# Two order edits in a transformer trunk: when the attention output is loaded and split, and where one variance product stands on TensorE

## The chip, the cores and the metric

The kernel runs on one core of one Trainium2 chip. Times are device microseconds (us) of one launch. A kernel is timed as the median of several runs; where a profile is read, the rows come from one profiled execution with a span of its own.

## What is computed

One inference step of two layers over 1,032 token columns (1,024 prompt positions and 8 decoding rows), with a model width of 1,024. Each layer is a token mixer, a layer norm, a gated feed-forward part with a causal convolution of width 3, and a second layer norm:

```python
xp = layer_norm(ALPHA * xp + hp, ln_g[i, 0], ln_b[i, 0])      # hp = attention output @ w_o (+ b_o in layer 1)
fp, sp = conv_ffn(xp, zeros_prev, w_up[i], conv_w[i], conv_b[i], w_down[i])
xp = layer_norm(ALPHA * xp + fp, ln_g[i, 1], ln_b[i, 1])

def layer_norm(x, g, b):
    xf = x.astype(jnp.float32)
    mu = xf.mean(-1, keepdims=True)
    var = jnp.square(xf - mu).mean(-1, keepdims=True)
    return ((xf - mu) * lax.rsqrt(var + LN_EPS) * g + b).astype(x.dtype)
```

Everything behind the mixer is called the trunk here. It runs twice, once for each layer; both edits are in it.

## The kernel before

**Arithmetic.** Every large product is made of three passes. Each operand is split into a rounded high part and the rest: ScalarE copies the high part (`w_hi`, `t_h_hi`, `x_hi`), VectorE or GpSimd subtracts it to get the low part (`w_lo`, `t_h_lo`, `x_lo`), and TensorE adds high times high, high times low and low times high in PSUM (lines 101 to 103, in the helper `product`). The model dimension lies on partitions, the tokens on the free axis, in three chunks of 352, 352 and 328 columns (`CHUNKS`, c = 0, 1, 2).

**Blocks.** The trunk is a list of blocks (`trunk_slots`, `slots`). Block b multiplies one weight piece of 128 x 1024 with one chunk: 8 x 3 matmuls. Blocks 0 to 23 are the output projection `w_o`, kind "o": blocks 0 to 7 are chunk 0 (m = 0 to 7), 8 to 15 chunk 1, 16 to 23 chunk 2. Block 24 is the first of the feed-forward part; it reads the normalised chunk 0. All engines walk through the same list, each with its own instructions in program order; semaphores join them.

**Weights.** `raw`, `w_hi` and `w_lo` are rings of three slots (`RING`). SyncE issues the load of block b (`load_w`, line 1288, 512 KB) once the low part of block b - 3 is done. In its block b, ScalarE first copies the high part of block b + 2 (line 1337), once TensorE has finished block b - 1. GpSimd makes the low parts of even blocks (line 1455), VectorE those of odd blocks (line 1536, in its block b for block b + 2, b odd).

**Attention output.** The mixer leaves it in DRAM (`o_scr`). For every chunk it is loaded in four quarters q = 0 to 3 of 128 x 2 x 352 values (`load_o`, line 1279) into staging columns, and each quarter is split by ScalarE (line 1342) and VectorE (line 1542). The four staging places are the same for every chunk, so the load of quarter q of chunk c waits until quarter q of chunk c - 1 is split:

```python
need(sp, s_olo, 4 * (c - 1) + q + 1)      # line 1278, on SyncE's queue
```

Before the change, the loads of chunk c + 1 stand behind `load_w` at m = 5 of chunk c (line 1301), and all four splits stand in ScalarE's and VectorE's block m = 6 (lines 1424 and 1670).

**Norm steps.** When the eight tiles of a chunk are projected, its layer norm is worked off beside the blocks of the next chunk. `NORM` lists its steps with an offset, and `norm_block(stage, what, at)` gives the block; stage 0 is chunk 0 behind the output projection, which ends with block 7, so `end` is 8. For stage 0: the mean product on TensorE ahead of block 10 (line 1770); "center" k = 0 to 3 on VectorE in blocks 10 to 13 (line 1604) and "square" k on ScalarE right behind in the same block (lines 1376 and 1381); the sums of squares on VectorE ("add", line 1611, blocks 12 to 14, "fold", line 1616, block 15); the variance product on TensorE (line 1774), square root on ScalarE (line 1387) and reciprocal on VectorE (line 1621), all with block 16; then "scale" (VectorE, line 1627), "high" (ScalarE, line 1401), "affine" (GpSimd, line 1488) and "low" (VectorE, line 1633), k = 0 to 3, one block apart, from blocks 17, 17, 18 and 19. Block 24 waits for all four "low".

Within a block, ScalarE does: weight copy, quarter copies if any, norm steps. VectorE does: weight split (odd b), quarter splits if any, norm steps, then the residual addition of the tile of block b - 1 (lines 1559 and 1562). GpSimd does its weight split (even b), adds the tile to the running sum (line 1470), then norm steps.

Of the kernel before, what the change touches and what calls it, by code (L numbers as in the profile page):

```python
# [50 lines left out]
NCH = len(CHUNKS)  # L51
# [4 lines left out]
def f32(ap):  # L56
    return ap.bitcast(F32)


def need(eng, sem, count):  # L60

    if isinstance(count, int) and count <= 0:
        return
    eng.wait_ge(sem, count)
# [1033 lines left out]
def stage_of(kind, c):  # L1098
    return c if kind == "o" else NCH + c


def stage_end(stage):


    return KT * (stage + 1) if stage < NCH else NCH * KT + FFN_BLOCKS * (stage - NCH + 1)
# [11 lines left out]
def norm_block(stage, what, at):  # L1117


    end = stage_end(stage)  # L1120
    if what == "mean":
        return end + 2 + (10 if stage == 2 else 0)
    if stage == 0:
        return end + 2 + at
    if what == "affine":
        at += 0.5
    return (26, 50)[stage - 1] + int(2 * at) if stage < NCH else end + 2 + int(2 * at)
# [11 lines left out]
def mixer_b_constants(zb):  # L1139


    views, at = {}, 0
    flat = zb[:, :, :].rearrange("p m c -> p (m c)")
    for name, size in (("cos", T), ("sin", T), ("mask", 2 * P), ("ident", P), ("nsink", NH), ("bias", 3 + PAIRS)):
        views[name] = flat[:, at:at + size]
        at += size
    return views


def trunk(nc, x_hi, x_lo, banks, ring, zb, dram, layer):  # L1150
# [5 lines left out]
    with ctx:  # L1156
# [62 lines left out]
        def pieces(b):  # L1219
            kind, c, m, j = slots[b]  # L1220
            return DOWN_PIECES[j] if kind == "d" else KT
# [17 lines left out]
        def stored(stage):  # L1239

            return final and stage >= NCH

        def o_part(c, q):


            n = CHUNKS[c][1]
            stage = (h_hi, h_lo)[q // 2][:, 16 + 2 * (q % 2):18 + 2 * (q % 2), 0:n]
            a = 8 * (c % 2) + 2 * q
            return f32(stage), h_hi[:, a:a + 2, 0:n], h_lo[:, a:a + 2, 0:n]
# [7 lines left out]
        def two(ap, k, n):  # L1257


            return ap[:, 2 * k:2 * k + 2, 0:n]  # L1260
# [4 lines left out]
        @block.sync  # L1265
        def _(sp):
            def source(kind, m, j):
                if kind == "o":
                    return dram["w_o"][m]
                if kind in "gu":  # L1270
                    return dram["w_up"][2 * m + j]
                if kind == "p":
                    return dram["w_b"][AHEAD[m]]
                return dram["w_down"][3 * m + j]

            def load_o(c, q):
                off, n = CHUNKS[c]
                need(sp, s_olo, 4 * (c - 1) + q + 1)
                sp.dma_start(o_part(c, q)[0],
                             dram["o_scr"].rearrange("(m p) t -> p m t", p=P)[:, 2 * q:2 * q + 2, off:off + n]  # L1280
                             ).then_inc(o_in[q], 16)

            def load_w(b):
                kind, c, m, j = slots[b]
                n = pieces(b) * P
                if b >= RING:
                    need(sp, s_wlo[b % 2 if RING % 2 == 0 else 1 - b % 2], (b - RING) // 2 + 1)
                sp.dma_start(raw[:, b % RING, 0:n], source(kind, m, j)[:, 0:n]).then_inc(w_in[b % RING], 16)

            load_w(0)  # L1290
            for q in range(4):
                load_o(0, q)
            if biased:
                sp.dma_start(bias[:, :], dram["bias_o"]).then_inc(s_bias, 16)
            for b in range(1, n_blocks):
                kind, c, m, j = slots[b]
                load_w(b)
                if b == 3:
                    for dst, name in ((state[:, :, :, :], "state"), (taps[:, :, :], "taps"), (ln[:, :, :, :], "ln")):
                        sp.dma_start(dst, dram[name][layer]).then_inc(s_const, 16)  # L1300
                if kind == "o" and m == 5 and c + 1 < NCH:
                    for q in range(4):
                        load_o(c + 1, q)
                if stored(stage_of("d", c - 1)) and kind == "g" and m == 14:
                    store_y = c - 1
                    off, n = CHUNKS[store_y]
                    need(sp, s_y, KT * (NCH + store_y + 1))
                    sp.dma_start(dram["yT"].rearrange("(m p) t -> p m t", p=P)[:, :, off:off + n],
                                 z[(NCH + store_y) % 2][:, :, 0:n]).then_inc(s_out, 16)
            if not final:  # L1310
                views = mixer_b_constants(zb)
                sp.wait_ge(s_blk, N_BLOCKS)
                for part, name in (("cos", "cos"), ("sin", "sin"), ("mask", "mask_b"), ("ident", "ident"), ("bias", "bias_b")):
                    sp.dma_start(views[part], dram[name]).then_inc(s_next, 16)
                sp.dma_start(views["nsink"], dram["sinks"].partition_broadcast(P)).then_inc(s_next, 16)
            need(sp, s_save, NCH * FT)
            sp.dma_start(dram["gT"][layer], gtail[:, :, :]).then_inc(s_out, 16)
            if final:
                off, n = CHUNKS[NCH - 1]
                for k in range(KT // 2):  # L1320
                    need(sp, s_y, KT * (N_STAGES - 1) + k + 1)
                    need(sp, s_yodd, k + 1)
                    sp.dma_start(two(dram["yT"].rearrange("(m p) t -> p m t", p=P)[:, :, off:off + n], k, n),
                                 two(z[(N_STAGES - 1) % 2], k, n)).then_inc(s_out, 16)
            need(sp, s_out, 16 * (1 + NCH - 1 + KT // 2 if final else 1))
            if not final:
                sp.wait_ge(s_next, 16 * 6)

        @block.scalar
        def _(act):  # L1330
# [8 lines left out]
            def split_o(c, q):  # L1339
                src, hi, _ = o_part(c, q)  # L1340
                act.wait_ge(o_in[q], 16 * (c + 1))
                act.copy(hi, src).then_inc(s_ohi, 1)
# [75 lines left out]
            for b in range(n_blocks):  # L1418
                kind, c, m, j = slots[b]
                if b + 2 < n_blocks:  # L1420
                    split(b + 2)
                if biased and tile_before(b) and tile_before(b)[0] == "o":
                    add_bias(b, *tile_before(b)[1:])
                if kind == "o" and m == 6 and c + 1 < NCH:
                    for q in range(4):
                        split_o(c + 1, q)
                if kind == "g" and m > 1:
                    high_h(c, m - 2)
                if kind == "u":
                    gate_rows(b, c, m)  # L1430
                    if m > 0:
                        silu(c, m - 1)
                if kind == "d" and m == 0 and j == 0:
                    silu(c, FT - 1)
                    high_h(c, FT - 2)
                if kind == "d" and m == 0 and j == 1:
                    high_h(c, FT - 1)
                if b == 8:
                    act.wait_ge(s_const, 48)
                for stage, what, k in norm_steps(b):  # L1440
                    norm(stage, what, k)
# [89 lines left out]
        def _(dve):  # L1531
# [7 lines left out]
            def split_o(c, q):  # L1539
                src, hi, lo = o_part(c, q)  # L1540
                dve.wait_ge(s_ohi, 4 * c + q + 1)
                dve.tensor_tensor(lo, src, f32(hi), ALU.subtract).then_inc(s_olo, 1)  # L1542
# [123 lines left out]
            for b in range(n_blocks):  # L1666
                kind, c, m, j = slots[b]
                if b % 2 == 1 and b + 2 < n_blocks:
                    split(b + 2)
                if kind == "o" and m == 6 and c + 1 < NCH:  # L1670
                    for q in range(4):
                        split_o(c + 1, q)
                if kind == "u":
                    convolve(c, m)
                    if m > 0:
                        gate(b - 1, c, m - 1)
                if kind == "d" and m == 0 and j == 0:
                    gate(b, c, FT - 1)
                if b == 8:
                    dve.wait_ge(s_const, 48)  # L1680
                if b == ROWS_AT:
                    sample_rows()
                for stage, what, k in norm_steps(b):
                    norm(stage, what, k)
                for tile in tile_due(b):
                    residual(*tile)
# [963 lines left out]
```

## Time and profile before

| | us |
|---|---|
| median of 3 runs | 3184.15 (3181.24 to 3186.31) |
| the profiled execution, its own time | 3190.73 |
| its span | 3189.1 |
| TensorE busy in the span | 3086.4 (97%) |
| VectorE, ScalarE, GpSimd busy | 1598.9, 1528.1, 1542.6 (50%, 48%, 48%) |
| mean granted TensorE clock | 0.984 of full |

TensorE is busy nearly all the time, so the time of the kernel is TensorE's work plus the places where it stands still; about 100 us of the span are such places. "Idle" in a row is time in which an engine had nothing to run, with the instruction that ended it. A clock of 1.00 in a row is 2.4 GHz, 0.50 is 1.2 GHz.

### The profile page before, as it was taken

The page shows a single profiled execution, that of the slowest core. Times are in us where ns is not written, and L with a number is a line of the kernel's source. Part 1 is how long each engine was busy: PE and PEld are TensorE (multiplying, and loading weights), DVE is VectorE, ACT ScalarE, POOL GpSimd, SP SyncE. Part 2 cuts the span into 40 slices and gives each one's busy share as a digit, 9 for nine tenths or more (in the row PEclk, how much of TensorE's full clock was granted, in tenths as well). Part 3 has the DMA queues.
Part 4 walks back from the last instruction along what each step waited for, and adds up shares of the span by engine and source line. Part 5 has one row for each costly group of instructions (what it writes and reads, how often), then busy time and mean ns, then how long its engine had stood idle before and what let it go on. Part 6 is the DMA issues. An engine that isn't in the chain of part 4 may idle for free. (4 is left out here: it accounts for less than half of the span.)

```text
span 3189.1 us, 54992 instructions
## 1 busy us (share of the span) xinstructions
PE 3086.4 (97%) x21141; PEld 2974.7 (93%) x21141; DVE 1598.9 (50%) x3409; ACT 1528.1 (48%) x3235; POOL 1542.6 (48%) x1277
## 2 busy tenths in 40 slices
PE   8999999999999889999999999999899999999997
PEld 8999999999999859999999999988799999999997
DVE  3234434344343446664463465589756653433543
ACT  4555555555555424553453353367655543533542
POOL 4344443444444315665564465454256654554663
PEclk9999999999999989999999999999899999999998
DMA  6676676776776474444444444311244444444542
GB/s 225 241 262 229 226 259 230 244 258 209 267 256 222 173 289 137 144 134 128 137 133 141 137 144 143 119 37 43 79 164 134 140 128 136 156 133 143 163 145 96
DMA packets 134212, 540.80 MB, mean 170 GB/s; under 512 B 24336, under 2 KB 48544, under 8 KB 131120
## 3 DMA queue, kind: packets, MB, share of 16 engines
q1 hardware_dynamic: 133440, 536.51, 50.0%
q8 instruction: 169, 2.77, 0.4%
q14 instruction: 91, 0.75, 0.1%
q0 software_dynamic: 224, 0.26, 0.0%
q10 hardware_dynamic: 288, 0.52, 0.0%
HBM read 497.55 MB, written 216.85 MB: 224 GB/s over the span
## 5 line engine op out<-in xcount | busy, mean ns | idle before, releaser
L1337 ACT CAST w_hi<-raw 128x1024 fp32r<-128x1024 f32 (+1 forms) x459 | 471.5, 1027 | 847.7 <-PE bank L103 796.9
L101 PE MATMUL bank<-x_hi,w_hi 128*128 128x352 f32 (+1 forms) x2208 | 711.9, 322 | 5.6 <-POOL w_lo L1455 4.3
L102 PE MATMUL bank<-x_lo,w_hi 128*128 128x352 f32 (+1 forms) x2208 | 705.9, 320 | 0.0
L103 PE MATMUL bank<-x_hi,w_lo 128*128 128x352 f32 (+1 forms) x2208 | 702.5, 318 | 0.0
L1536 DVE TENSOR_TENSOR w_lo<-raw,w_hi 128x1024 fp32r<-128x1024 f32 (+1 forms) x229 | 320.2, 1398 | 737.7 <-ACT w_hi L1337 737.7
L1455 POOL TENSOR_TENSOR w_lo<-raw,w_hi 128x1024 fp32r<-128x1024 f32 (+1 forms) x230 | 546.8, 2378 | 277.0 <-ACT w_hi L1337 277.0
L101 PE MATMUL a_gemm<-x_hi,a_w_hi 128*128 128x352 f32 (+1 forms) x1728 | 561.0, 325 | 11.2 <-DVE x_lo L645 11.2
L102 PE MATMUL a_gemm<-x_lo,a_w_hi 128*128 128x352 f32 (+1 forms) x1728 | 553.7, 320 | 0.0
L103 PE MATMUL a_gemm<-x_hi,a_w_lo 128*128 128x352 f32 (+1 forms) x1728 | 551.7, 319 | 0.0
L101 PE MATMUL bank<-t_h_hi,w_hi 128*128 128x352 f32 (+1 forms) x1440 | 465.0, 323 | 7.9 <-POOL t_h_lo L1475 5.7
L103 PE MATMUL bank<-t_h_hi,w_lo 128*128 128x352 f32 (+1 forms) x1440 | 463.4, 322 | 0.0
L102 PE MATMUL bank<-t_h_lo,w_hi 128*128 128x352 f32 (+1 forms) x1440 | 460.6, 320 | 0.0
L101 PEld LDWEIGHTS bank<-x_hi,w_hi 128*128 128x128 f32 x2208 | 414.7, 188 | 8.7 <-POOL w_lo L1455 5.3
L102 PEld LDWEIGHTS bank<-x_lo,w_hi 128*128 128x128 f32 x2208 | 415.3, 188 | 1.6
L103 PEld LDWEIGHTS bank<-x_hi,w_lo 128*128 128x128 f32 x2208 | 415.0, 188 | 0.0
L577 POOL TENSOR_TENSOR a_w_lo<-a_raw,a_w_hi 128x1024 fp32r<-128x1024 f32 x72 | 172.3, 2392 | 387.3 <-ACT a_w_hi L445 387.3
L101 PEld LDWEIGHTS a_gemm<-x_hi,a_w_hi 128*128 128x128 f32 x1728 | 326.1, 189 | 13.5 <-issue 9.1
L102 PEld LDWEIGHTS a_gemm<-x_lo,a_w_hi 128*128 128x128 f32 x1728 | 326.5, 189 | 0.0
L103 PEld LDWEIGHTS a_gemm<-x_hi,a_w_lo 128*128 128x128 f32 x1728 | 325.7, 188 | 0.0
L736 DVE CUSTOM_DVE_ANT_0 a_sp<-a_scores,a_mask 128x128 f32<-128x128 f32 (+1 forms) x384 | 112.2, 349 | 357.8 <-PE a_scores L895 357.8
L1475 POOL TENSOR_TENSOR t_h_lo<-t_acc,t_h_hi 128x352 fp32r<-128x352 f32 (+1 forms) x132 | 128.9, 976 | 332.9 <-ACT t_h_hi L1359 332.9
L101 PEld LDWEIGHTS bank<-t_h_hi,w_hi 128*128 128x128 f32 x1440 | 273.8, 190 | 10.4 <-issue 6.9
(292 smaller groups left out, 5055.3 us busy)
## 6 DMA issues: line engine op xcount, KB each, us to landing
raw<-w_up SPq DMA_DIRECT2D x264, 512.0 KB, 3.7
roll<-cache SPq DMA_DIRECT2D x128, 1023.5 KB
raw<-w_down SPq DMA_DIRECT2D x96, 512.0 KB, 3.5
a_raw<-w_a SPq DMA_DIRECT2D x72, 512.0 KB, 3.6
roll<-cache SPq DMA_DIRECT2D x16, 2044.0 KB
raw<-w_o SPq DMA_DIRECT2D x48, 512.0 KB, 3.6
raw<-w_down SPq DMA_DIRECT2D x48, 384.0 KB, 3.5
vT<-a_vt SPq DMA_DIRECT2D x24, 516.0 KB, 5.2
```

The lines of the kernel that those rows point to most:

```text
L101: pe.matmul(out, w_hi, x_hi, start=first, stop=False)
L102: pe.matmul(out, w_hi, x_lo, start=False, stop=False)
L103: return pe.matmul(out, w_lo, x_hi, start=False, stop=last)
L577: pool.tensor_tensor(w_lo[:, b % 2], raw[:, b % 2], f32(w_hi[:, b % 2]), ALU.subtract).then_inc(s_wlo, 1)
L736: dve.tensor_tensor_reduce(out=sp[:, u % 2, j, h, w0:], in0=s_bank[h][:, 2 * P * j + w0:2 * P * (j + 1)], in1=mk, scale=1.0, scalar=3.0e38 ...
L1337: act.copy(w_hi[:, b % RING, cols], raw[:, b % RING, cols]).then_inc(s_whi, 1)
L1455: pool.tensor_tensor(w_lo[:, b % RING, cols], raw[:, b % RING, cols], f32(w_hi[:, b % RING, cols]), ALU.subtract).then_inc(s_wlo[0], 1)
L1475: pool.tensor_tensor(h_lo[:, m, 0:n], acc[:, unit(c, m) % 3, 0:n], f32(h_hi[:, m, 0:n]), ALU.subtract).then_inc(s_hlo, 1)
L1536: dve.tensor_tensor(w_lo[:, b % RING, cols], raw[:, b % RING, cols], f32(w_hi[:, b % RING, cols]), ALU.subtract).then_inc(s_wlo[1], 1)
```

## The change

Three edits, the same in both trunk calls.

```diff
     if stage == 0:
-        return end + 2 + at
+        return end + 2 + at + (1 if what == "var" else 0)
@@ SyncE
-                if kind == "o" and m == 5 and c + 1 < NCH:
+                if kind == "o" and m == 1 and c + 1 < NCH:
                     for q in range(4):
                         load_o(c + 1, q)
@@ ScalarE, and the same on VectorE
-                if kind == "o" and m == 6 and c + 1 < NCH:
-                    for q in range(4):
-                        split_o(c + 1, q)
+                if kind == "o" and 2 <= m < 6 and c + 1 < NCH:
+                    split_o(c + 1, m - 2)
```

The loads of the next chunk's quarters stand behind `load_w` of blocks 1 and 9 in place of 5 and 13. The quarters are split in blocks 2, 3, 4, 5 and 10, 11, 12, 13, one in each, in place of four in block 6 and four in block 14. The variance product of stage 0 stands ahead of block 17 in place of block 16; square root and reciprocal keep their place on ScalarE and VectorE. The later code lies one or two lines higher: line 1774 becomes 1772, 1542 becomes 1541.

SyncE's DMA issues from the start of the first trunk, before the change (`w_o0` is the first layer's `w_o`, `t0_h_hi` and `t0_h_lo` hold the staging places):

```order
L1288 DMA raw<-w_o0 128x1024
L1279 DMA t0_h_hi<-o_scr 128x2x352 x2
L1279 DMA t0_h_lo<-o_scr 128x2x352 x2
L1288 DMA raw<-w_o0 128x1024 x3
L1300 DMA t0_state<-state 128x352
L1300 DMA t0_taps<-taps 128x88
L1300 DMA t0_ln<-ln 128x32
L1288 DMA raw<-w_o0 128x1024 x2
L1279 DMA t0_h_hi<-o_scr 128x2x352 x2
L1279 DMA t0_h_lo<-o_scr 128x2x352 x2
```

And with it:

```order
L1288 DMA raw<-w_o0 128x1024
L1279 DMA t0_h_hi<-o_scr 128x2x352 x2
L1279 DMA t0_h_lo<-o_scr 128x2x352 x2
L1288 DMA raw<-w_o0 128x1024
L1279 DMA t0_h_hi<-o_scr 128x2x352 x2
L1279 DMA t0_h_lo<-o_scr 128x2x352 x2
L1288 DMA raw<-w_o0 128x1024 x2
L1300 DMA t0_state<-state 128x352
L1300 DMA t0_taps<-taps 128x88
L1300 DMA t0_ln<-ln 128x32
```

The four loads of chunk 1 now stand ahead of the weight loads of blocks 2 and 3, not behind that of block 5.

VectorE in blocks 10 to 13 of the first trunk, before the change, from the first "center" (bank 6 holds the mean):

```order
L1604 TENSOR_TENSOR zb<-zb,bank6 128x704
L1559 SCALAR_TENSOR_TENSOR bank3<-x_hi,bank3 128x352
L1562 SCALAR_TENSOR_TENSOR t0_z<-x_lo,bank3 128x352
L1536 TENSOR_TENSOR w_lo<-raw,w_hi 128x1024
L1604 TENSOR_TENSOR zb<-zb,bank6 128x704
L1559 SCALAR_TENSOR_TENSOR bank4<-x_hi,bank4 128x352
L1562 SCALAR_TENSOR_TENSOR t0_z<-x_lo,bank4 128x352
L1611 TENSOR_TENSOR t0_sums2<-t0_sums2,t0_sq 128x704
L1604 TENSOR_TENSOR zb<-zb,bank6 128x704
```

And with it:

```order
L1541 TENSOR_TENSOR t0_h_lo<-t0_h_hi 128x2x328
L1603 TENSOR_TENSOR zb<-zb,bank6 128x704
L1558 SCALAR_TENSOR_TENSOR bank3<-x_hi,bank3 128x352
L1561 SCALAR_TENSOR_TENSOR t0_z<-x_lo,bank3 128x352
L1535 TENSOR_TENSOR w_lo<-raw,w_hi 128x1024
L1541 TENSOR_TENSOR t0_h_lo<-t0_h_hi 128x2x328
L1603 TENSOR_TENSOR zb<-zb,bank6 128x704
L1558 SCALAR_TENSOR_TENSOR bank4<-x_hi,bank4 128x352
L1561 SCALAR_TENSOR_TENSOR t0_z<-x_lo,bank4 128x352
L1541 TENSOR_TENSOR t0_h_lo<-t0_h_lo,t0_h_hi 128x2x328
L1610 TENSOR_TENSOR t0_sums2<-t0_sums2,t0_sq 128x704
L1603 TENSOR_TENSOR zb<-zb,bank6 128x704
```

Each "center" now has a quarter split ahead of it.

TensorE around the variance product of stage 0, before the change (bank 3 is block 15, bank 4 block 16):

```order
L101 MATMUL bank3<-t0_h_hi,w_hi 128x352
L102 MATMUL bank3<-t0_h_lo,w_hi 128x352
L103 MATMUL bank3<-t0_h_hi,w_lo 128x352
L1774 MATMUL bank7<-t0_sums2,t0_mean_w 128x352
L101 MATMUL bank4<-t0_h_hi,w_hi 128x328
```

And with it:

```order
L101 MATMUL bank4<-t0_h_hi,w_hi 128x328
L102 MATMUL bank4<-t0_h_lo,w_hi 128x328
L103 MATMUL bank4<-t0_h_hi,w_lo 128x328
L1772 MATMUL bank7<-t0_sums2,t0_mean_w 128x352
L101 MATMUL bank5<-t0_h_hi,w_hi 128x328
```

The product stands behind block 16 and ahead of block 17.

## Rows read from the trace of the kernel before

**Rows 1.** The page: span; groups of instructions (busy us, mean ns, idle before).

```profile
span 3189.1 us, 54992 instructions
...
L1337 ACT CAST w_hi<-raw 128x1024 fp32r<-128x1024 f32 (+1 forms) x459 | 471.5, 1027 | 847.7 <-PE bank L103 796.9
...
L1455 POOL TENSOR_TENSOR w_lo<-raw,w_hi 128x1024 fp32r<-128x1024 f32 (+1 forms) x230 | 546.8, 2378 | 277.0 <-ACT w_hi L1337 277.0
```

**Rows 2.** Waits of TensorE (us in total, times, longest us).

```profile
PE bank L1774 <- DVE t_sums L1616: 14.6, 3, 6.4
```

**Rows 3.** Timeline of TensorE (start us, us, instruction, idle before).

```profile
1183.00 0.32 PE L101 MATMUL bank<-t_h_hi,w_hi 128*128 128x352 f32 x1
...
1229.68 0.32 PE L101 MATMUL bank<-t_h_hi,w_hi 128*128 128x352 f32 x1
...
1233.49 0.32 PE L101 MATMUL bank<-t_h_hi,w_hi 128*128 128x352 f32 x1
...
1241.64 1.54 PE L1774 MATMUL bank<-t_sums,t_mean_w 128*128 128x352 f32 x2 [4.17 <-DVE t_sums L1616]
...
1247.54 0.31 PE L101 MATMUL bank<-t_h_hi,w_hi 128*128 128x328 f32 x1
...
1274.92 0.40 PE L101 MATMUL bank<-x_hi,w_hi 128*128 128x352 f32 x1 [1.42 <-POOL w_lo L1455]
...
2376.08 1.54 PE L1774 MATMUL bank<-t_sums,t_mean_w 128*128 128x352 f32 x2 [4.05 <-DVE t_sums L1616]
...
2382.97 0.31 PE L101 MATMUL bank<-t_h_hi,w_hi 128*128 128x328 f32 x1
```

**Rows 4.** Timeline of TensorE, a stall at 1456 us and the block behind it.

```profile
1456.63 0.56 PE L101 MATMUL bank<-t_h_hi,w_hi 128*128 128x352 f32 x1 [2.49 <-POOL t_h_lo L1475]
...
1462.12 0.32 PE L101 MATMUL bank<-t_h_hi,w_hi 128*128 128x352 f32 x1
```

**Rows 5.** Stretches of TensorE (us, busy, granted clock, DMA share, GB/s).

```profile
1242.00:1244.00 2.00, 2.00 (x6) 0.50 0.56 209
1275.00:1277.00 2.00, 2.00 (x13) 1.00 0.78 258
```

**Rows 6.** Timelines at the first trunk's start: SyncE, VectorE, GpSimd.

```profile
1169.37 4.91 SPq L1288 DMA_DIRECT2D raw<-w_o  x3
...
1175.39 1.74 DVE L1542 TENSOR_TENSOR t_h_lo<-t_h_lo,t_h_hi 128x704 fp32r<-128x704 f32 x2
...
1179.10 2.40 POOL L1455 TENSOR_TENSOR w_lo<-raw,w_hi 128x1024 fp32r<-128x1024 f32 x1 [5.19 <-ACT w_hi L1337]
```

**Rows 7.** From issue to landing: weight loads at 1178 to 1180, at 1183.91.

```profile
DMA to landing us min/median/max: 3.4/3.4/3.4
...
DMA to landing us min/median/max: 7.4/7.4/7.4
```

**Rows 8.** Timelines of VectorE, GpSimd and ScalarE in block 6.

```profile
1200.27 3.32 DVE L1542 TENSOR_TENSOR t_h_lo<-t_h_hi 128x704 fp32r<-128x704 f32 x2 [2.27 <-ACT t_h_hi L1342]
...
1199.64 2.41 POOL L1455 TENSOR_TENSOR w_lo<-raw,w_hi 128x1024 fp32r<-128x1024 f32 x1 [0.60 <-ACT w_hi L1337]
...
1199.46 1.46 ACT L1342 CAST t_h_hi<-t_h_hi 128x704 fp32r<-128x704 f32 x2
```

**Rows 9.** Timelines of VectorE and GpSimd in blocks 10 to 14.

```profile
1214.62 0.89 DVE L1604 TENSOR_TENSOR zb<-zb,bank 128x704 f32<-128x704 f32 x1 [0.83 <-PE bank L1770]
...
1219.57 1.23 DVE L1536 TENSOR_TENSOR w_lo<-raw,w_hi 128x1024 fp32r<-128x1024 f32 x1 [3.06 <-ACT w_hi L1337]
...
1214.96 2.40 POOL L1455 TENSOR_TENSOR w_lo<-raw,w_hi 128x1024 fp32r<-128x1024 f32 x1 [1.35 <-ACT w_hi L1337]
...
1232.14 2.40 POOL L1455 TENSOR_TENSOR w_lo<-raw,w_hi 128x1024 fp32r<-128x1024 f32 x1
```

**Rows 10.** Timeline of VectorE behind the variance product.

```profile
1243.81 2.35 DVE L1621 RECIPROCAL t_rstd<-t_rstd 128x352 f32<-128x352 f32 x1 [1.23 <-ACT t_rstd L1387]
...
1250.02 1.69 DVE L1627 TENSOR_TENSOR zb<-zb,t_rstd 128x704 f32<-128x704 f32 x2
```

More of the change, by code:

```diff
@@ L1669, in _ @@
                     split(b + 2)
-                if kind == "o" and m == 6 and c + 1 < NCH:
-                    for q in range(4):
-                        split_o(c + 1, q)
+                if kind == "o" and 2 <= m < 6 and c + 1 < NCH:
+                    split_o(c + 1, m - 2)
                 if kind == "u":
```

## The prediction

> **What bounds the kernel now.** The page comes first: a span of 3189.1 us [rows 1], with TensorE busy for 97% of it. So only TensorE's standing still can change the time. The waits of TensorE come second: the longest total inside the trunk belongs to the variance product, L1774, 14.6 us in three times, each ended by VectorE's `t_sums` [rows 2]. Third, TensorE's timeline shows where [rows 3]: 4.17 us at 1241.64 and 4.05 us at 2376.08, ahead of block 16 of either trunk. (The third, 6.4 us, stands at the kernel's end and isn't touched.) The granted clock costs more on top. After the stall it is 0.50, which is 1.2 GHz [rows 5]. A block of chunk 1 takes 3.81 us (1229.68 to 1233.49), one of chunk 2 328/352 of it, 3.6 us, and the product some 0.6 us. From the product to block 17 it should be 4.2 us, and it was 5.90 and 6.89 us [rows 3]. So the two variance stalls cost 4.17 + 1.70 and 4.05 + 2.69, together 12.6 us. That is all the change can win there. Block 24 waited another 1.42 us, at 1274.92 [rows 3], as its own weights and the four "low" of chunk 0 allow. The row names GpSimd's weight split, but block 24 also waits for the last "low", which VectorE does in block 22, behind seven steps that hang on the variance; I read that as what ended the wait. So behind the variance there is a chain with no slack at all towards block 24, and this decides the change.
>
> **Part 1: the early load on SyncE.** The quarter loads of chunk 1 now stand behind `load_w(1)`, and each waits until the same quarter of chunk 0 is split on VectorE. These splits run until 1175.39 + 1.74 = 1177.13 [rows 6]. SyncE issues in order, so `load_w(2)`, issued at about 1169.9 before (second of the three at 1169.37 [rows 6]), now goes out behind the fourth quarter load, at about 1177.7, 7.8 us later. Until it lands: the shortest landing of such a load is 3.4 us. The longest, 7.4 us, is that of the load that stood right behind four quarter loads issued within 2 us [rows 7]. Here the four go out over about 3 us, paced by VectorE, and the pipe ahead of them is emptier, so I take 5.3 us, in the middle of the two: it lands at 1183.0. Then ScalarE's copy takes 1.03 us and GpSimd's split 2.38 us [rows 1], with 0.15 us between them: the low part is ready at 1186.5. Before, it was ready at 1179.10 + 2.40 = 1181.5 [rows 6], and block 2 began at 1183.00 [rows 3]. So 1.5 us of the delay are hidden, and TensorE stands still for 3.5 us. Bounds: 1.7 us with a landing of 3.4, 5.7 with 7.4. Blocks 3 and 4 have room behind it, since the ring fills while TensorE waits.
>
> What a stall of 3.5 us does to the clock: behind one of 2.49 us the next block took 5.49 us (1456.63 to 1462.12) for 3.85, 1.6 us more [rows 4]. Behind 4.17 and 4.05 it was 1.7 and 2.7 us. Behind 1.42 us the clock stayed at 1.00 [rows 5]. I take 1.6 us. The second trunk has the same order, so the same again: 2 x (3.5 + 1.6) = **+10.2 us**. At blocks 9 and 10 the same wait on SyncE costs nothing: its weight loads run a good two blocks ahead there, and no split queues behind a missing load. If that cover went, it would be about 1.4 us.
>
> **Part 2: the quarters in blocks 10 to 13.** What goes: ahead of the last "add" in block 14 VectorE no longer runs four splits (in block 6 the first two took 3.32 us [rows 8], two without company 1.74 [rows 6]), the cause of the stall at block 16. What comes: a copy of 0.7 us on ScalarE and a split on VectorE ahead of every "center". In block 6 a pair of splits took 3.32 us, where two take 1.74 [rows 6, 8]. GpSimd's weight split ran from 1199.64 to 1202.05, and the pair ended at 1203.59, 1.5 us later. Two splits need 1.74, so nearly all of both ran behind GpSimd's end: the first stood still until GpSimd was through, and ended 0.75 us behind it. In even blocks the quarter again meets GpSimd's split, 0.7 us after its start, the length of ScalarE's copy (1.46 us for two [rows 8]).
>
> The page SBUF — State Buffer of the Trainium skill (section "SBUF: two separate sides") says why: VectorE with two SBUF inputs and GpSimd share one port pair as an exclusive lock, and the later one fully blocks. By it a "center", with one input in PSUM, isn't held, as the 0.89 us at 1214.62 beside GpSimd's 1214.96 agrees [rows 9]. By the rule part 2 costs what follows; with unheld splits of 0.87 us it would be a gain, which is the first rival.
>
> Now the chain, in times of the trace before. Block 10: GpSimd's split ends at 1214.96 + 2.40 = 1217.4 [rows 9], the quarter 0.75 us later, "center" 0 ends at 1218.9 (before 1215.5), "square" 0 at 1219.8. ScalarE takes the copy for block 13 only then: 1220.8. Block 11: weight split 1.2 us (1219.57 was its start before [rows 9]), quarter, "center" 1 at 1223.6, "square" 1224.4, next copy 1225.4. Block 12: one running sum and the weight split on GpSimd until 1228.0, quarter 1228.8, "add" 1, "center" 2 at 1230.3, "square" 1231.2, copy 1232.2. Block 13: weight split 1233.5 (block 15 begins at 1233.49, just met), quarter, "add" 2, "center" 3 at 1235.9, "square" 1236.8, copy for block 16 at 1237.8, GpSimd's split of it at 1240.3. Before, this split began at 1232.14 [rows 9]. Block 16 is due at 1233.49 + 3.81 = 1237.3, so a **new stall of 3.0 us** takes the place of the old one, now on `w_lo` from GpSimd, and costs the clock 1.6 us.
>
> **Part 3: the variance product one block later.** It no longer waits: the fold is ready at about 1242. It runs behind block 16, at 1240.4 + 3.6 + 1.6 = 1245.6, for 1241.64 before. At full clock the reciprocal follows 1.4 us later, at 1247.0, for 1243.81 before [rows 10]. Then come the reciprocal 2.35, a residual 1.05 and a weight split 1.2 us, so "scale" 0 begins at 1251.5, for 1250.02 before [rows 10]; before, VectorE was free at 1243.81 + 2.35 + 1.05 = 1247.2 and its weight split began only 1.2 us ahead of 1250.02, so a wait of 1.6 us for a copy falls away. So the norm's second half is 1.5 us later, and with it block 24, since the chain ends with it: **+1.5 us** a trunk, 3.0 in all. All the 12.6 us on TensorE are used up by the time it stands still again: at block 16, about 1 us ahead of block 18 (the mean of stage 1 needs the residual that is queued behind the reciprocal), and some 2.8 us at block 24. This last stall lies near the 2.49 us that lowered the clock, and I charge 1.6 us for one of the two trunks: **+1.6 us**.
>
> **The sum.** 10.2 + 3.0 + 1.6 = +14.8 us. The profiled execution took 3190.73 us, 6.6 more than the median, with the same work in it, so the difference is put on the median: 3184.15 + 14.8 = 3199 us. About 0.2%, 6.4 us, is what a measurement of this kernel can tell from no change.
>
> **The rivals.**
> - *The quarters aren't held by GpSimd.* Then each costs 0.87 us, the split for block 16 is ready at about 1237.7, the product runs at 1241.3 at full clock, and "scale" 0 begins at about 1247.2, 2.8 us earlier than before. The sum is 10.2 - 5.6 + 1.6 = +6.2: 3190 us. The 3.32 us of [rows 8] speak against it. Chance 0.15.
> - *The clock doesn't fall at the new stalls.* That takes away 3.2 (block 2), 3.2 (block 16) and 1.6 (block 24): +6.8, 3191 us. With the landing of 3.4 us it is +3.2, 3187 us. The stall of 1.42 us speaks for it, the one of 2.49 against. Chance 0.20.
> - *Faster: the second half of the norm follows TensorE's blocks and not itself.* Its weight splits do wait for TensorE's blocks, as the 1.6 us before "scale" 0 show. Were every step ahead of block 24 paced so, the 12.6 us would be won, and with landings of 3.4 us and no lower clock part 1 would take back 2 x 1.7: -9.2, 3175 us. It decides once "scale" 0 begins by more than 5 us earlier than 1250.02. Against it: block 24 waited already before. Chance 0.04.
> - *The load isn't early at all.* It does nothing for the loads of chunk 1, whose first wait is VectorE's; this is part 1 itself.
>
> **How the numbers follow.** The forecast, with smaller and larger landings and clocks, has 0.61. Its own range is 3190 to 3207: the landing of 7.4 us in both trunks adds 4.4, clocks of 2.7 for 1.6 us some 4. The low bounds of all terms together give +3.3 - 5.6 = -2.3, 3182 us, the high ones about +27, 3211 us; neither end is likely in all terms at once, so the range is 3184 to 3207. Slower by over 0.2%: the forecast and about 0.18 of the first two rivals, 0.79. Within: 0.17. Faster: 0.04.
>
> **What would show it.** SyncE's second `raw<-w_o` issue moves to about 1177.7. A wait of about 3.5 us stands at block 2, on GpSimd's `w_lo`, and another of about 3 us at block 16, with L1772 waiting for nothing. Clock 0.50 follows either. L1541 in blocks 10 and 12 takes about 2 us or more. Block 24 waits nearly 3 us. Wrong would be: no wait at block 2 (the loads don't queue as I say), or no wait at block 16 together with "scale" 0 well ahead of its old place.

## The result, and the profile after

| | us | to the kernel before |
|---|---|---|
| median, before (5 runs) | 3185.91 (3181.24 to 3186.31) | |
| median, changed (5 runs) | 3198.88 (3197.16 to 3202.14) | 1.0048, 95% interval 1.0036 to 1.0060 |
| profiled execution, changed: own time, span | 3198.88, 3197.3 | before: 3190.73, 3189.1 |

The change makes the kernel slower by 0.5%, some 15 us by the ratio (11 to 19); the two medians lie 13.0 us apart. The forecast was 3199.0.

A line of the changed kernel's page, first section; TensorE is still busy for 96% of the span:

```profile
PE 3082.3 (96%) x21141; PEld 2971.7 (93%) x21141; DVE 1602.7 (50%) x3409; ACT 1526.9 (48%) x3235; POOL 1537.2 (48%) x1277
```

TensorE's waits (us in total, times, longest), first one of the kernel before, then three of the changed kernel:

```profile
PE bank L101 <- POOL w_lo L1455: 4.3, 4, 1.4
```

```profile
PE bank L101 <- POOL w_lo L1454: 20.0, 8, 4.2
...
PE bank L1768 <- POOL t_sums L1469: 6.7, 3, 2.3
PE bank L1772 <- DVE t_sums L1615: 6.4, 1, 6.4
```

Against [rows 2], the variance product (now L1772) has lost both waits in the trunks; what is left is the 6.4 us at the kernel's end. But the waits for GpSimd's `w_lo` grew from 4.3 us in four times to 20.0 us in eight. TensorE's timeline of the changed kernel says where (start, duration, operation, in brackets the idle time before it and what ended it):

```profile
1184.98 0.66 PE L101 MATMUL bank<-t_h_hi,w_hi 128*128 128x352 f32 x1 [4.19 <-POOL w_lo L1454]
...
1244.20 0.41 PE L101 MATMUL bank<-t_h_hi,w_hi 128*128 128x328 f32 x1 [3.11 <-POOL w_lo L1454]
...
1247.92 0.75 PE L1772 MATMUL bank<-t_sums,t_mean_w 128*128 128x352 f32 x2
...
1254.61 0.86 PE L1768 MATMUL bank<-t_sums,t_mean_w 128*128 128x352 f32 x2 [2.31 <-POOL t_sums L1469]
...
1279.49 0.40 PE L101 MATMUL bank<-x_hi,w_hi 128*128 128x352 f32 x1 [2.26 <-POOL w_lo L1454]
...
1462.73 0.40 PE L101 MATMUL bank<-t_h_hi,w_hi 128*128 128x352 f32 x1 [2.48 <-POOL t_h_lo L1474]
...
2322.45 0.66 PE L101 MATMUL bank<-t_h_hi,w_hi 128*128 128x352 f32 x1 [3.96 <-POOL w_lo L1454]
...
2383.03 0.64 PE L101 MATMUL bank<-t_h_hi,w_hi 128*128 128x328 f32 x1 [3.10 <-POOL w_lo L1454]
...
2388.26 0.75 PE L1772 MATMUL bank<-t_sums,t_mean_w 128*128 128x352 f32 x2
...
2419.56 0.40 PE L101 MATMUL bank<-x_hi,w_hi 128*128 128x352 f32 x1 [2.15 <-POOL w_lo L1454]
```

In order: block 2, block 16, the variance product, block 18's mean and block 24 of the first trunk; then a stall far behind them, which [rows 4] show before the change with the same length; then blocks 2, 16 and 24 of the second trunk. Two waits of the kernel before (the 4.17 us and 1.42 us of [rows 3]) have become four in each trunk. The clock of the same places, TensorE in stretches of 2 us (bounds, length, busy time and instructions, granted clock, DMA share, GB/s):

```profile
1186.00:1188.00 2.00, 2.00 (x8) 0.50 0.73 262
1246.00:1248.00 2.00, 2.00 (x15) 1.00 0.91 354
1281.00:1283.00 2.00, 2.00 (x9) 0.50 0.30 100
1464.00:1466.00 2.00, 2.00 (x15) 1.00 0.28 115
2324.00:2326.00 2.00, 2.00 (x8) 0.50 0.95 311
2384.00:2386.00 2.00, 2.00 (x9) 0.50 0.84 277
2421.00:2423.00 2.00, 2.00 (x9) 0.50 0.46 119
```

And a stretch of the kernel before, in the block behind its stall at 1456.63:

```profile
1458.00:1460.00 2.00, 2.00 (x9) 0.50 0.32 129
```

**A measure free of the rest of the kernel.** I count from the keep-busy matmuls at a trunk's start (1166.89 and 2301.37 before, 1164.97 and 2302.65 after) to the mean product of block 36, which lies behind all that the change touches. Before, it is 154.36 and 155.22 us; after, 162.38 and 164.77: +8.0 and +9.6, together +17.6 us. Behind the stall at 1462.73 (the first down-projection block) some comes back. Before the change the clock fell to 0.50 there, and the block took 5.49 us [rows 4]; now it stays at 1.00 behind the same 2.48 us, and the block takes 3.89. Counted to the next mean product (1543.32 before, 1546.78 after in the first trunk), 2.6 and 2.1 us come back, 1.6 of it in that block of either trunk. What remains is +12.9. The two profiled spans differ by 8.2 only; the other 4.7 us lie where nothing was changed, 1.9 of them before the first trunk begins. So single spans say little to a few us; the ratio of the runs, and this measure, say more.

### The profile page after: what moved, and what is told of

It is laid out like the page before. It is cut to its first block and busy times, and to the rows that moved or that the text cites. A ratio compares the mean times of both kernels' runs of the same rounds, so it can differ in the third digit from the quotient of the medians.

```text
span 3197.3 us, 54992 instructions
## 1 busy us (share of the span) xinstructions
PE 3082.3 (96%) x21141; PEld 2971.7 (93%) x21141; DVE 1602.7 (50%) x3409; ACT 1526.9 (48%) x3235; POOL 1537.2 (48%) x1277
```

## The experiments

The theory: three separate effects. (1) The early loads delay `load_w(2)` on SyncE, and block 2 stands still. (2) The quarter splits ahead of each "center" are held by GpSimd's weight split, and the split for block 16 is late. (3) Moving the variance product wins next to nothing, since the chain of the norm sets block 24. The rivals: the splits aren't held and only their number counts; the product's later place is itself what costs.

The table gives the change and all eleven experiments. "Trunk" is the sum of the two marks above against the kernel before, from one profile each.

| kernel | median, us | ratio (95%) | trunk, us |
|---|---|---|---|
| changed | 3198.88 | 1.0048 (1.0036 to 1.0060) | +17.6 |
| e1: before, loads early | 3210.58 | 1.0068 (1.0056 to 1.0081) | +19.9 |
| e2: changed, loads behind `load_w` of the third block | 3192.93 | 1.0019 (1.0010 to 1.0028) | +8.7 |
| e3: changed, product ahead of block 16 | 3202.49 | 1.0043 (1.0030 to 1.0056) | +13.2 |
| e4: changed, chunk 2's splits in block 14 | 3193.65 | 1.0021 (1.0012 to 1.0030) | +10.7 |
| e5: changed, quarters at the block's end | 3197.03 | 1.0035 (1.0022 to 1.0047) | +11.9 |
| e6: changed, chunk 2's quarters in blocks 11, 13 | 3195.16 | 1.0035 (1.0022 to 1.0049) | +7.6 |
| e7: before, product ahead of block 17 | 3181.10 | 0.9989 (0.9981 to 0.9998) | -4.0 |
| e8: e2, e3 and e5 together | 3188.53 | 1.0010 (1.0001 to 1.0019) | +2.2 |
| e10: chunk 2's quarters in block 9, product ahead of 16 | 3181.19 | 0.9989 (0.9980 to 0.9998) | -4.8 |
| e11: e10, product ahead of 17 | 3182.67 | 0.9989 (0.9980 to 0.9997) | -0.8 |
| e12: e7, with root and reciprocal a block later | 3181.99 | 0.9986 (0.9977 to 0.9995) | -3.8 |

**e1, the early load alone**, in the kernel before:

```diff
-                if kind == "o" and m == 5 and c + 1 < NCH:
+                if kind == "o" and m == 1 and c + 1 < NCH:
                     for q in range(4):
                         load_o(c + 1, q)
```

> Only the early load: loads of the next chunk at m = 1, splits and variance product as before the change. My theory (the load holds back the weights of block 2): the whole wait of about 4 us plus a slower clock of 1.8 to 2.8 us appears at block 2 of both trunks, and nothing else changes, so about +12.7 us on the kernel before: 3198 us, which is all of the change's loss. Rival (the loss comes from the quarter splits in blocks 10 to 13, and block 2's wait only moves a later one): 3186 to 3190 us. A third view, that the wait at block 2 adds only its idle time and not the clock: +8 us, 3194 us.

Measured: 3210.58 us, by the medians slower than the whole change; the intervals of the two ratios overlap a little. The place was right, the size wrong. TensorE's timeline of e1 in the first trunk:

```profile
1188.38 0.66 PE L101 MATMUL bank<-t_h_hi,w_hi 128*128 128x352 f32 x1 [4.32 <-POOL w_lo L1455]
...
1223.85 0.83 PE L1770 MATMUL bank<-t_sums,t_mean_w 128*128 128x352 f32 x2 [2.82 <-POOL t_sums L1470]
```

The second row is new: 2.82 us at block 10's mean (2.66 in the second trunk). SyncE in the same kernel (start, duration, DMA), and ScalarE's next weight copy:

```profile
1209.97 1.18 SPq L1279 DMA_DIRECT2D t_h_hi<-o_scr  x2
1211.58 1.16 SPq L1279 DMA_DIRECT2D t_h_lo<-o_scr  x2
1212.78 2.05 SPq L1288 DMA_DIRECT2D raw<-w_o  x3
```

```profile
1218.31 1.05 ACT L1337 CAST w_hi<-raw 128x1024 fp32r<-128x1024 f32 x1 [7.73 <-DMA raw<-w_o]
```

With the splits left in block 6, the loads for chunk 2 stand behind block 9's weights but wait until chunk 1's quarters are split in block 6, which takes VectorE until 1212.35. Every weight load behind them waits too; three then go out together. In the change the quarters of chunk 1 are split from block 2 on, so this second hold is absent. An early load and its early use belong together.

**e2, the loads one block later in the change:** `m == 1` becomes `m == 2`, so that `load_w(2)` goes out ahead of them.

> The change with the loads at m = 2 in place of m = 1, so that the weights of block 2 are issued ahead of them; the weights of block 3 go out late but have a block more room. My theory: no wait at block 2 or 3, all else as in the change, so 12.7 us less than the change: about 3186 us, the time before. Rival (the delay passes on to block 3): a wait of 1 to 3 us there and 3190 to 3195 us.

Measured: 3192.93, about 9 us less than the change by the ratios, for 12.7 expected. Block 2 waits for nothing. The waits of e2 in the first trunk:

```profile
1238.27 0.64 PE L101 MATMUL bank<-t_h_hi,w_hi 128*128 128x328 f32 x1 [3.11 <-POOL w_lo L1454]
...
1250.04 0.86 PE L1768 MATMUL bank<-t_sums,t_mean_w 128*128 128x352 f32 x2 [2.32 <-POOL t_sums L1469]
...
1274.99 0.40 PE L101 MATMUL bank<-x_hi,w_hi 128*128 128x352 f32 x1 [2.48 <-POOL w_lo L1454]
```

The wait at block 16 has the same 3.11 us as in the change, but now the clock falls behind it in the first trunk too (0.64 us for its first matmul, 0.41 in the change). The trunk measure gives -8.9 as well. So theory (1) holds. I read the rest of the 12.7 in block 16's clock, in slightly longer waits at block 24 (2.48 and 2.40 us) and in small new waits at block 6 (0.78 and 0.51).

**e3, the product back ahead of block 16 in the change** (the first edit undone):

> The change with the variance product ahead of block 16 again. My theory (the norm's chain sets when block 24 starts, so TensorE's place of the product is worth nothing there): the wait of 3.1 us at block 16 becomes one of about 5.4 us on the fold, but block 24 waits less, and the kernel stays within 3 us of the change: 3196 to 3202 us. Rival (TensorE's stalls simply add up, and the edit saves its stall): 2.3 us more idle and 1.7 us of clock in each trunk, +8 us: 3207 us.

Measured: 3202.49, with a ratio whose interval overlaps the change's. The trunk measure is 4.4 us lower, and most of that is clock: block 24 takes 3.93 us in both trunks, for 5.47 and 5.48 in the change. But behind the mark the first down-projection block takes 5.42 and 5.46 us, for 3.89 in the change, which cancels most of it. So the later place of the product costs nothing that the whole kernel shows. TensorE's timeline of e3:

```profile
1247.88 1.54 PE L1772 MATMUL bank<-t_sums,t_mean_w 128*128 128x352 f32 x2 [5.40 <-DVE t_sums L1615]
...
1281.02 0.40 PE L101 MATMUL bank<-x_hi,w_hi 128*128 128x352 f32 x1 [1.42 <-POOL w_lo L1454]
```

One wait of 5.40 us holds what the change spreads over 3.11 and 2.31, and block 24 waits 1.42 as in [rows 3].

**e4, chunk 2's four splits back in block 14:**

```diff
-                if kind == "o" and 2 <= m < 6 and c + 1 < NCH:
+                if kind == "o" and 2 <= m < 6 and c == 0:
                     split_o(c + 1, m - 2)
+                if kind == "o" and m == 6 and c == 1:
+                    for q in range(4):
+                        split_o(c + 1, q)
```

> The change with only chunk 2's four quarter splits back in block 14; chunk 1's stay spread over blocks 2 to 5, the early load and the moved variance product stay. My theory (the quarters ahead of the center steps delay the norm's first half): the wait for the low part of block 16's weights goes, the reciprocal starts earlier, block 24 comes some 3.9 us earlier in each trunk than in the change (2.4 us ahead of before in place of 1.5 us behind), and the sum is 3199 - 8 = 3191 us; the clock at block 24 can add or take 3 us. Rival (block 2's wait is the whole loss and the place of chunk 2's quarters is worth nothing): 3199 us.

Measured: 3193.65, for 3191 expected, the wait at block 16 gone, block 2 still 4.17 and 3.95 us. So the quarters in blocks 10 to 13 make block 16's wait. Whether by their work or by being held, e6 tells.

**e5, the quarters at the end of the block**, behind the norm steps:

> The change with each quarter's copy and split at the end of its block, behind the norm steps and the residual, in place of ahead of them; same blocks, same early load, variance product ahead of block 17. My theory (what hurts is that each center waits for a quarter held by GpSimd): no wait at block 16, as in the run with chunk 2's splits back in block 14, and the same time as that one, ratio 1.002 to the kernel before, 3192 us, of which block 2's wait is more than all. Rival (four more splits on VectorE and ScalarE in these blocks are too much work wherever they stand): the wait of 3 us at block 16 stays, 3199 us.

Measured: 3197.03, a miss. Block 16 still waits 1.13 and 0.89 us, and VectorE's timeline shows a hold that wasn't expected there:

```profile
1227.06 1.24 DVE L1541 TENSOR_TENSOR t_h_lo<-t_h_hi 128x656 fp32r<-128x656 f32 x1 [0.49 <-ACT t_h_hi L1342]
1228.22 3.09 DVE L1610 TENSOR_TENSOR t_sums<-t_sums,t_sq 128x704 f32<-128x704 f32 x1
```

The quarter got in ahead of GpSimd's weight split, which ran from 1228.05 to 1230.55, and the "add" behind it, 0.88 us elsewhere, took 3.09. Why the ratio is no better than 1.0035 isn't settled.

**e6, the same quarters in pairs, in the odd blocks**, where GpSimd has no weight split:

```diff
-                if kind == "o" and 2 <= m < 6 and c + 1 < NCH:
+                if kind == "o" and 2 <= m < 6 and c == 0:
                     split_o(c + 1, m - 2)
+                if kind == "o" and m in (3, 5) and c == 1:
+                    split_o(c + 1, m - 3)
+                    split_o(c + 1, m - 2)
```

> The change with chunk 2's quarters in pairs in blocks 11 and 13, where GpSimd has no weight split, still ahead of the center steps; chunk 1 as in the change. The work is the same, only the meeting with GpSimd's 2.4 us split goes. My theory (GpSimd's hold of about 1.8 us in each of blocks 10 and 12 makes the wait at block 16): the splits take 0.8 us each in place of 2.6, the wait at block 16 falls from 3.1 us to 0 to 0.5 us, 3192 to 3194 us. Rival (it is the work itself, however long each split takes): the wait stays at 2.5 to 3 us, 3198 us.

Measured: 3195.16. In the trace (of the fastest of its runs, 3192.90) block 16 waits 0.54 us in either trunk, for 3.11 and 3.10 in the change, so nearly all of the wait is gone. VectorE's timeline, first of the changed kernel, then of e6:

```profile
1225.50 0.83 DVE L1541 TENSOR_TENSOR t_h_lo<-t_h_hi 128x656 fp32r<-128x656 f32 x1
...
1229.56 2.65 DVE L1541 TENSOR_TENSOR t_h_lo<-t_h_lo,t_h_hi 128x656 fp32r<-128x656 f32 x1 [1.44 <-ACT t_h_hi L1342]
```

```profile
1225.21 1.59 DVE L1544 TENSOR_TENSOR t_h_lo<-t_h_hi 128x656 fp32r<-128x656 f32 x2
...
1233.59 2.33 DVE L1544 TENSOR_TENSOR t_h_lo<-t_h_lo,t_h_hi 128x656 fp32r<-128x656 f32 x2
```

The operation and size are the same. In block 11 one takes 0.83 us, in block 12 2.65; in e6 two take 1.59 in block 11. The pair in block 13 took 2.33, beside a GpSimd addition that ran until 1234.47. GpSimd in the changed kernel beside block 12's:

```profile
1229.10 2.41 POOL L1454 TENSOR_TENSOR w_lo<-raw,w_hi 128x1024 fp32r<-128x1024 f32 x1
```

It ends at 1231.51, and the quarter 0.70 us behind it, at 1232.21. So the same work costs block 16 half a us in place of 3.1 when it doesn't meet GpSimd's weight split, and theory (2) is shown. The median is lower than the change's by 3.7 us, with overlapping intervals.

**e7, the product's move alone**, in the kernel before:

```diff
-        return end + 2 + at
+        return end + 2 + at + (1 if what == "var" else 0)
```

> The kernel before with only the variance product ahead of block 17. My theory (the norm's chain sets block 24): the 4.2 and 4.1 us ahead of the product fall to under 1 us and their slow clock goes, but 2.3 us come back ahead of block 18 and block 24 waits 2.5 us with a slower clock behind it, so 3181 to 3186 us, within 0.15% of before. Rival (the stalls were TensorE's loss and go for good): 12.6 us less, 3173 us.

Measured: 3181.10, ratio 0.9989. The product waits 0.23 us, for 4.17 and 4.05 before, and some 4 us come out of the 12.6 that these two waits cost. Block 24 waits 1.11 and 1.55 us at full clock, less than the 2.5 expected; the wait ahead of block 18 and the clock behind it take the larger part. TensorE's timeline of e7:

```profile
1246.00 1.54 PE L1770 MATMUL bank<-t_sums,t_mean_w 128*128 128x352 f32 x2 [2.34 <-POOL t_sums L1470]
...
1271.18 0.40 PE L101 MATMUL bank<-x_hi,w_hi 128*128 128x352 f32 x1 [1.11 <-POOL w_lo L1455]
```

**e8, the repairs together:** `m == 2`, quarters at the block's end, product ahead of block 16.

> Loads at m = 2, quarters at the end of blocks 2 to 5 and 10 to 13, variance product back ahead of block 16. My theory: no wait at block 2; square sums and fold are ready before block 16, so the product waits for nothing there and the norm's second half starts about 6 us earlier than in the kernel before; block 24 waits 1 to 1.5 us as before at full clock. The 12.6 us of the two variance stalls are won: 3173 us, ratio 0.996. Rival (the second half of the norm, from the square root on, is too long by itself, so the early product only makes block 24 wait longer): 3180 to 3185 us.

Measured: 3188.53, a clear miss. The variance product waits 5.05 and 4.93 us again. VectorE's and GpSimd's timelines of e8:

```profile
1224.85 3.08 DVE L1610 TENSOR_TENSOR t_sums<-t_sums,t_sq 128x704 f32<-128x704 f32 x1
...
1235.69 1.23 DVE L1541 TENSOR_TENSOR t_h_lo<-t_h_lo,t_h_hi 128x656 fp32r<-128x656 f32 x1 [0.50 <-ACT t_h_hi L1342]
1236.84 3.07 DVE L1610 TENSOR_TENSOR t_sums<-t_sums,t_sq 128x704 f32<-128x704 f32 x1
```

```profile
1224.69 2.49 POOL L1454 TENSOR_TENSOR w_lo<-raw,w_hi 128x1024 fp32r<-128x1024 f32 x1 [0.46 <-ACT w_hi L1337]
...
1236.68 2.47 POOL L1454 TENSOR_TENSOR w_lo<-raw,w_hi 128x1024 fp32r<-128x1024 f32 x1 [0.46 <-ACT w_hi L1337]
```

Each held "add" starts 0.16 us behind GpSimd's start. Moving the quarter didn't remove the hold, it handed it to the next operation with two SBUF inputs.

**e10 and e11, all four quarters of chunk 2 in block 9**, ahead of the "centers"; chunk 1 loads at m = 2, chunk 2 at m = 1. e10 has the product ahead of block 16, e11 ahead of 17.

```diff
-                if kind == "o" and m == 5 and c + 1 < NCH:
+                if kind == "o" and m == 2 - c and c + 1 < NCH:
...
-                if kind == "o" and m == 6 and c + 1 < NCH:
+                if kind == "o" and 2 <= m < 6 and c == 0:
+                    split_o(c + 1, m - 2)
+                if kind == "o" and m == 1 and c == 1:
                     for q in range(4):
                         split_o(c + 1, q)
```

> Chunk 1's loads behind the weight load of block 2 and its quarters in blocks 2 to 5; chunk 2's loads behind the weight load of block 9 and all its quarters in block 9, ahead of the first center and with no weight split of GpSimd in that block; variance product ahead of block 16. My theory (a norm step of chunk 0 on VectorE must not meet GpSimd's split, and the norm's start decides block 24): no wait at block 2, the sums are folded by the end of block 15, so under 1 us ahead of the product, block 24 waits 1 to 1.5 us, 3173 us, ratio 0.996. Rival (the delay of block 9's residual and of the first center by 2 us runs on through the whole norm): 1 to 3 us at the product, 3178 to 3184 us.

> As the run with all of chunk 2's quarters in block 9, but the variance product ahead of block 17 as in the change. My theory (the product's place on TensorE only delays the norm's second half when the sums are ready in time): the product comes a block, 3.6 to 4 us, later; 2.3 us stand ahead of block 18 and block 24 waits 2 us or more with a slower clock after it, so 4 to 6 us more than with the product ahead of block 16: 3178 us. Rival (the place makes no difference): the same time as that run.

Measured: 3181.19 and 3182.67, both with ratio 0.9989: better than both kernels, short of the 3173 hoped for, and no difference between them. In e10's second trunk the product waited for nothing, but block 24 waited 2.36 us; in the first the product still waited, because the weight split ahead of the "fold" was held (VectorE's timeline, then TensorE's):

```profile
1237.30 3.29 DVE L1538 TENSOR_TENSOR w_lo<-raw,w_hi 128x1024 fp32r<-128x1024 f32 x1
1240.51 1.24 DVE L1618 TENSOR_TENSOR t_sums<-t_sums 128x352 f32<-128x352 f32 x1
```

```profile
1241.81 1.36 PE L1778 MATMUL bank<-t_sums,t_mean_w 128*128 128x352 f32 x2 [2.20 <-DVE t_sums L1618]
```

**e12, e7 with square root and reciprocal a block later too** (`what in ("var", "dev", "inverse")`):

> The kernel before with the variance product, the square root and the reciprocal of stage 0 all one block later, so that the residual of block 15 no longer stands behind the reciprocal on VectorE. My theory (block 24 is set by the norm's chain): the 2.3 us ahead of block 18 go, the first scale begins about 1.3 us earlier than with the product moved alone, but TensorE only reaches block 24 sooner and waits about 3 us there in place of 1.1 to 1.5, with a slower clock behind it: 3178 to 3182 us, within 0.1% of the run with the product moved alone. Rival (stalls simply add): 2.3 us and the slow clock behind them are won in each trunk, 8 us: 3173 us.

Measured: 3181.99, ratio 0.9986, the same as e7. The wait ahead of block 18 shrank from 2.34 to 1.78 us, and block 24's grew from 1.11 and 1.55 to 2.40 and 2.30.

## Why the prediction was right

The time, 3199.0 for 3198.88, and the direction came out as forecast. Not all terms did; some misses cancel. The near-equality is partly luck of the base too: the forecast stood on a median of 3184.15, and the median before over five runs is 3185.91, so 13.0 us were measured by medians and 15 by the ratio, for 14.8. Up to the mark at block 36 the forecast's three terms came out as 11.8, 2.7 and 3.1 us, for 10.2, 3.0 and 1.6.

- **Part 1, +10.2.** Block 2 stood still for 4.19 and 3.96 us, for 3.5 forecast, since the load landed 5.8 us after its issue, for 5.3, on SyncE's second weight load behind the four quarters (all as described). In the second trunk the load landed after 5.6 us. The block then took 1.6 and 2.8 us longer, for 1.6. At block 10's mean product the trunks are 5.3 and 6.5 us late: 11.8 for 10.2. e2, which undoes this part, gains 9. Its mechanism is shown, its term a little low. The prediction's upper bound was read wrong: 7.4 us is not the longest landing of the trace before, since `load_w(2)` itself, issued at 1169.9, landed 8.1 us later.
- **The wait on SyncE at blocks 9 and 10.** Free in the change, as said. The number given for its cover gone, 1.4 us, was wrong: e1 takes the cover away, and each trunk has 2.8 us of wait there.
- **Part 2, a wait of 3.0 at block 16.** 3.11 and 3.10 us. In the first trunk the quarters in blocks 10 and 12 took 2.56 and 2.65 us, in the second 2.13 and 2.19, and each ended 0.7 us behind GpSimd's split; those in blocks 11 and 13 took 0.83; e6 shows that the meeting with GpSimd is the cause and e4 that the quarters are. That is the exclusive lock of the Trainium skill (page SBUF — State Buffer, section "SBUF: two separate sides"); these rows agree, the "adds" of e5 and e8 too. The rival that the quarters aren't held is refuted. The clock's 1.6 us was charged in both trunks and fell due in the second only.
- **Part 3, +3.0.** The product waited for nothing. Counted from block 10's mean product, block 24 starts 1.2 and 1.5 us later than before, together 2.7, for 1.5 each. That the last "low", and not the weight split that the row names, ends block 24's wait was only read in the prediction. VectorE's and GpSimd's rows of the changed kernel bear it out:

```profile
1276.35 3.04 DVE L1632 TENSOR_TENSOR x_lo<-zb,x_hi 128x704 fp32r<-128x704 f32 x1 [2.25 <-POOL zb L1487]
```

```profile
1276.28 2.36 POOL L1454 TENSOR_TENSOR w_lo<-raw,w_hi 128x1024 fp32r<-128x1024 f32 x1
```

  The weight split ends at 1278.64 and the "low" at 1279.39; block 24 starts at 1279.49. In all 26 trunks of the thirteen kernels the "low" ends 0.1 us ahead of block 24, and from the first "low" to block 24 it is 16.8 to 17.2 us. This last "low" starts right behind GpSimd's split and takes 3.03 to 3.07 us, where the one before it takes 0.89 (1272.26). So some 2 us of hold stand just ahead of block 24 in every kernel here, and no run tried to remove them.
  "Scale" 0 doesn't always follow the reciprocal. In the kernel before, e1, e3 and e8 it starts 5.3 us ahead of block 19 in each trunk, while the time from the reciprocal to block 24 varies from 31.0 to 32.2 us. In the kernel before it stands behind VectorE's weight split at 1248.88, which waited 1.74 us for ScalarE's copy at 1247.79, and that one 4.02 us for TensorE. So there the chain hangs in part on TensorE's blocks, which the prediction left to its rival of the faster kernel. e7 shows that the 12.6 us were not to be had by this edit: it gives 4. In the change the part is worth about what it takes; e3, without it, has the same ratio within the intervals.
- **Ahead of block 18, about 1.** 2.31 us measured, in both trunks; it isn't a term of the sum, since block 24 comes after it. What was mis-sized is what follows the reciprocal: I counted the residual, and not GpSimd's addition of the tile behind it, which took 1.84 us where it takes 0.93 elsewhere (1247.49). VectorE's and GpSimd's timelines of the changed kernel:

```profile
1249.30 2.35 DVE L1620 RECIPROCAL t_rstd<-t_rstd 128x352 f32<-128x352 f32 x1 [1.89 <-ACT t_rstd L1387]
...
1252.55 1.22 DVE L1535 TENSOR_TENSOR w_lo<-raw,w_hi 128x1024 fp32r<-128x1024 f32 x1
```

```profile
1247.49 0.93 POOL L1469 TENSOR_TENSOR t_sums<-t_sums,t_z 128x352 f32<-128x352 f32 x1 [1.46 <-DVE t_z L1561]
...
1252.71 1.84 POOL L1469 TENSOR_TENSOR t_sums<-t_sums,t_z 128x352 f32<-128x352 f32 x1 [1.93 <-DVE t_z L1561]
```

  VectorE's weight split started 0.16 us ahead of it and ended at 1253.77; the addition ended at 1254.55, and the mean product of block 18 began at 1254.61. I read it as the same hold the other way round; no run tested it.
- **Block 24, 2.8 with the clock falling once.** 2.26 and 2.15 us, with the clock at 0.50 behind both. Its length was near, its clock, 1.5 us in each trunk, charged once too few.
- **Not foreseen:** the 4.7 us given back at the first down-projection block, where the clock stays up now. It offsets that part 1 and the clock at block 24 were counted too low. So the sum was right partly by luck; the two main stalls, at block 2 and block 16, were right by mechanism and nearly by size.

A faster kernel was a rival with 0.04, and needed the norm paced by TensorE's blocks. e7 and e12 decide against it: of 12.6 us about 4 were won, and the rest came back as waits and lower clock at blocks 18 and 24.

## What to carry to other kernels

A load put ahead of others on a queue that issues in order brings its own wait with it. Ask what is queued behind it and how much slack that has. Before a VectorE operation with two SBUF inputs is moved, look at what GpSimd runs at that moment; the hold falls on whichever such operation starts first behind GpSimd's, so moving one may only change the victim (e5, e8), and what took the wait at block 16 from 3.1 to 0.54 us is a place with no GpSimd weight split beside it (e6). And removing a wait wins only the slack of the chain behind it: follow that chain to its next consumer before counting the wait as a gain.

## What the runs showed that I had not expected

- **A stall's length alone doesn't decide the clock.** Behind 3.11 us at 1244.20 the granted clock read 1.00, behind 3.10 us at 2383.03 0.50, both at block 16 of the same kernel. Behind 2.26 and 2.15 us at block 24 it fell, and behind 2.30 to 2.39 us at the same block it stayed in the second trunks of e10, e11 and e12 (3.92 to 3.93 us for the block). Behind 2.48 us at the first down-projection block it fell in the kernel before and not in the changed one. Ahead of block 18 the pair took 0.86 us behind 2.31 in the change and 1.54 behind 2.34 in e7, as these stretches of the two agree (the change, then e7):

```profile
1255.00:1257.00 2.00, 2.00 (x14) 1.00 0.60 246
```

```profile
1246.00:1248.00 2.00, 2.00 (x5) 0.50 0.82 262
```

  Each fall costs 1.5 to 2.8 us, so two kernels alike in all waits can differ by several us. What decides it stays open.
- **The falls are not independent of each other.** In twelve of the 26 trunks block 18 or 24 took 5.4 us or more, for 3.9 at full clock, and in all twelve the first down-projection block, 46 or more blocks later, then took 3.9. In thirteen of the other fourteen it took 5.4 to 5.5; the exception is the second trunk of e10. So the 1.5 us that a fall costs at block 24 came back later, and of the 4.7 us above 3.2 lie in those two blocks. The runs don't show why.
- **The price of the hold.** An operation of 0.83 to 0.89 us that starts behind GpSimd's 2.4 us split took 2.13 to 3.09, in the main the longer the sooner it starts behind GpSimd's, and ended some 0.7 us behind GpSimd's end.
- **e10 and e11 are equal** though one has a wait at the variance product and the other at block 18. The best kernels found, e7, e10, e11 and e12, all lie 0.1% under the kernel before, and their intervals overlap; none of them is shown to be the best.
